# Fourth chunk of the input projection by seven half-sized products, with the first unit's exponentials, two weight sums and two tiles' taps moved behind it

## The reference

```python
h = rmsnorm(x, attn_norm_w)
proj = jnp.einsum('btd,de->bte', h, w_in)                 # 1024 -> 6400 columns
xin, bg, cg, q, k, v, g_conv, g_attn = jnp.split(proj, ...)
conv_out, conv_state = causal_short_conv(cg * xin, conv_prefix, conv_w)   # 3 taps in time
y_conv = bg * conv_out
q, k = rmsnorm(q, q_norm_w), rmsnorm(k, k_norm_w)
y_attn = window_attention(q, k, v, rel_bias, sinks)       # 16 heads, 2 of keys, window 128
merged = sigmoid(g_conv) * y_conv + sigmoid(g_attn) * y_attn
x = x + merged @ w_out
x = x + moe_ffn(rmsnorm(x, ffn_norm_w))                   # top 4 of 32 experts
```

## Time and profile before

| | |
|---|---|
| time of three runs | 1147.71, 1148.14 (median), 1148.73 us |
| the profiled execution: its own time | 1147.19 us |
| its span, first to last instruction | 1145.4 us |
| TensorE busy in the span | 1097.6 us (96%) |
| VectorE busy in the span | 437.5 us (38%) |
| mean granted TensorE clock | 0.993 |
| transfers | 444.36 MB, mean 388 GB/s |

### The profile page before, as it was taken

How to read it: one execution, slowest core, us unless ns; L and a number is a source line. 1 busy time by engine, 2 the same in 40 slices (tenths; PEclk the granted TensorE clock), 3 DMA queues, 4 the chain that set the end, 5 groups by cost and what they waited for, 6 DMA issues and landing times.

```text
span 1145.4 us, 15065 instructions
## 1 busy us (share of the span) xinstructions
PE 1097.6 (96%) x6055; PEld 497.1 (43%) x6055; DVE 437.5 (38%) x858; ACT 188.0 (16%) x398; POOL 88.4 (8%) x161
## 2 busy tenths in 40 slices
PE   9999999999999999999898999999999999999997
PEld 6689898543333333333333333333333333333332
DVE  4577786753433223233223232323232323232322
ACT  2133341221321101010101010101010101010101
POOL 1785215000000000000000000000000000000000
PEclk9999999999999999999999999999999999999999
DMA  9947629999999999999999999999999999999997
GB/s 313 314 128 186 210 85 353 416 357 425 400 420 426 419 432 431 430 433 431 433 433 429 434 430 433 435 428 434 429 434 431 431 434 429 435 429 434 425 423 287
DMA packets 53206, 444.36 MB, mean 388 GB/s; under 512 B 13101, under 2 KB 19373, under 8 KB 35741
## 3 DMA queue, kind: packets, MB, share of 16 engines
q1 hardware_dynamic: 46712, 435.83, 91.7%
q0 software_dynamic: 5600, 7.32, 2.4%
q10 hardware_dynamic: 852, 0.64, 0.2%
HBM read 439.78 MB, written 2.37 MB: 386 GB/s over the span
## 4 chain that ended last, share of the span: by engine, by line
PE 62%; DMA 37%; DVE 0%; issue 0%; ACT 0%; ACTq 0%; SPq 0%; DVEq 0%
PE pA L2051 32%; PE pB L2051 21%; DMA ring<-in_w_up 21%; DMA ring<-in_w_down 10%; PE pM L2051 6%; DMA area<-in_w_up 5%; PE pM L2054 1%; PE pA L2054 1%; DMA x<-in_x_prompt 1%; ACT area L1269 0%; DVE x L1898 0%; SPq L800 0%; DVE conv_row L1812 0%; DVE area L1973 0%; DVE x L1978 0%
## 5 line engine op out<-in xcount | busy, mean ns | idle before, releaser
L2051 PE MATMUL pA<-ring,hn 128*64 128x512 f32 x1536 | 352.6, 602 | 23.0 <-DMA ring<-in_w_up 23.0
L2051 PEld LDWEIGHTS pA<-ring,hn 128*64 128x64 f32 x1536 | 105.3, 137 | 218.8 <-issue 185.5
L2051 PE MATMUL pB<-ring,area 128*64 128x512 f32 (+2 forms) x784 | 171.5, 591 | 6.6 <-DMA ring<-in_w_down 5.8
L2051 PE MATMUL pA<-area,hn 128*64 128x512 f32 x512 | 119.3, 610 | 10.4 <-DMA area<-in_w_up 10.4
L2051 PE MATMUL pB<-area,ring 128*128 128x132 f32 (+2 forms) x928 | 126.4, 327 | 0.0
L2051 PEld LDWEIGHTS pB<-area,ring 128*128 128x128 f32 (+1 forms) x928 | 106.7, 175 | 18.2 <-issue 2.3
L2051 PEld LDWEIGHTS pB<-ring,area 128*64 128x64 f32 (+2 forms) x784 | 58.5, 136 | 101.2 <-issue 87.8
L1898 DVE TENSOR_TENSOR x<-pM,x 128x512 f32<-128x512 f32 x60 | 40.1, 691 | 147.7 <-PE pM L2051 147.7
L1257 ACT ACTIVATE area<-area 128x512 f32<-128x512 f32 x30 | 18.9, 631 | 385.2 <-DVE area L1881 385.2
L1812 DVE COPY conv_row<-pM 128x512 f32<-128x512 f32 x30 | 20.6, 686 | 146.0 <-PE pM L2051 146.0
L2051 PEld LDWEIGHTS pA<-area,hn 128*64 128x64 f32 x512 | 36.2, 139 | 74.5 <-issue 59.7
(11 more groups left out here) (348 smaller groups left out, 907.1 us busy)
## 6 DMA issues: line engine op xcount, KB each, us to landing
ring<-in_w_up SPq DMA_DIRECT2D x36, 4096.0 KB, 29.8
ring<-in_w_down SPq DMA_DIRECT2D x18, 4096.0 KB, 29.0
area<-in_w_up SPq DMA_DIRECT2D x12, 4096.0 KB, 30.2
ring<-in_w_up SPq DMA_DIRECT2D x16, 2048.0 KB, 13.4
area<-in_w_down SPq DMA_DIRECT2D x6, 4096.0 KB, 30.0
ring<-in_w_in SPq DMA_DIRECT2D x22, 1024.0 KB, 10.0
ring<-in_w_down SPq DMA_DIRECT2D x16, 1024.0 KB, 11.6
ring<-in_w_up SPq DMA_DIRECT2D x16, 1024.0 KB, 8.4
```

The lines of the kernel that those rows point to most:

```text
L2051: return pe.matmul(out, w, m, start=start, stop=stop, skip_group_check=True)
```

## The change

Chunk 4 (xin, first half) goes from four tiles to seven products. What goes with it:

```diff
-SEVEN = (3, 5, 6, 7, 9, 10, 11, 12)
-EARLY_SIDES = (3, 5)
+SEVEN = (3, 4, 5, 6, 7, 9, 10, 11, 12)
+EARLY_SIDES = (3, 4, 5)
...
-UNIT_STEPS = [(slot(3, 2), slot(3, 4), slot(3, 4), slot(3, 6), slot(3, 6), slot(5, 4), slot(5, 6)),
+UNIT_STEPS = [(slot(3, 2), slot(3, 4), slot(3, 4), slot(4, 0), slot(4, 2), slot(5, 4), slot(5, 6)),
...
-FIRST_TAP_STEPS = [15, 16, 17, 17, 30, 31, 32, 33]
-TAP_STEPS = [16, 17, slot(5, 0), slot(5, 0), 31, 32, 33, slot(9, 0)]
+FIRST_TAP_STEPS = [slot(4, 5), slot(4, 5), slot(4, 6), slot(4, 6), 30, 31, 32, 33]
+TAP_STEPS = [slot(4, 6), slot(4, 6), slot(5, 1), slot(5, 1), 31, 32, 33, slot(9, 0)]
...
-             5: (slot(3, 1), slot(3, 2), slot(3, 6), 14),
+             4: (slot(3, 1), slot(3, 2), slot(3, 4), slot(3, 6)),
+             5: (slot(4, 0), slot(4, 1), slot(4, 4), slot(5, 2)),
...
-    for n, what in ((15, "s_scores"), (16, "s_exp"), (17, "s_norm"), (slot(5, 3), "s_turn"), (slot(5, 5), "s_values")):
+    for n, what in ((slot(4, 2), "s_scores"), (slot(4, 4), "s_exp"), (slot(4, 6), "s_norm"), (slot(5, 3), "s_turn"), (slot(5, 5), "s_values")):
...
+                    if xin:
+                        out = quarter(cx[:, :, 2:], c, name)
+                        V.tensor_tensor(out, g, out, ALU.mult).then_inc(quarters_made, 1)
+                        dve.wait_ge(quarters_made, MADE_BEFORE[c] + ("c22", "c12", "c21").index(name) + 1)
```

More of the change, by code:

```diff
@@ L210, in plan @@
     after[2] += [("square", 0), ("qknorm", 0), ("bias_table", 0)]
-    for g, at in enumerate(((6, 7, 8, 9), (slot(3, 1), slot(3, 3), slot(3, 5), 14))):
+    for g, at in enumerate(((6, 7, 8, 9), (slot(3, 1), slot(3, 3), slot(3, 5), slot(4, 1)))):
         for n, what in enumerate((("q_sum", g), ("q_inverse", g), ("q_norm", (g, 0)), ("q_norm", (g, 1)))):
@@ L243, in plan @@
         after[SPLIT_STEPS[n]].append(("split", n))
+    assert not any(after[n] for n in range(len(TILES)) if TILES[n][1] in SEVEN)
     steps = [("anorm", 0), ("s_cols", 0)]
@@ L331, in counts @@
             for name in ("r1", "c11", "w", "c22", "c12", "c21"):
-                if name != "c11" or kind == "bg":
+                if name != "c11" or kind in ("bg", "xin"):
                     d += 1
@@ L347 @@
 counts()
+MADE_BEFORE = {4: 0, 8: 3 * (4 in SEVEN)}
 AFTER_XIN = [c for c in SEVEN if STEPS.index(("slot", (c, 0))) > STEPS.index(("sides", 4))]
@@ L600, in build @@
         tap_ready = sem("tap_ready")
+        quarters_made = sem("quarters_made")
         state_tapped = sem("state_tapped")
@@ L1110, in _ @@
                         act.wait_ge(kv_stored, 16 * 16)
-                    n = TILES.index(("xin", 4 if a < 4 else 8, a % 4, a))
-                    act.wait_ge(tile_free_dve, DVE_TILES[n] + 1)
+                    c = 4 if a < 4 else 8
+                    if c in SEVEN:
+                        act.wait_ge(quarters_made, MADE_BEFORE[c] + (2 if a % 4 < 2 else 3))
+                        act.wait_ge(tile_free_dve, DVE_READ[c, "c12"])
+                    else:
+                        act.wait_ge(tile_free_dve, DVE_TILES[TILES.index(("xin", c, a % 4, a))] + 1)
                     nc.scalar.activation(yc[:, a, 0:SEQ], cx[:, a, 0:SEQ], ACT.Copy,
@@ L1394, in place_of @@
                     return quarter(cx[:, :, 2:], c, name) if plain else g
+                xin = TILES[2 + 4 * (c - 1)][0] == "xin"
                 def times(name, g):
@@ L1399, in times @@
                     dve.wait_ge(tile_free_dve, DVE_READ[c, name])
-                    out = quarter(yc, c, name)
-                    link(V.tensor_tensor(out, g, out, ALU.mult))
+                    if xin:
+                        out = quarter(cx[:, :, 2:], c, name)
+                        V.tensor_tensor(out, g, out, ALU.mult).then_inc(quarters_made, 1)
+                        dve.wait_ge(quarters_made, MADE_BEFORE[c] + ("c22", "c12", "c21").index(name) + 1)
+                    else:
+                        out = quarter(yc, c, name)
+                        link(V.tensor_tensor(out, g, out, ALU.mult))
                 if s == 0:
@@ L1412, in seven @@
                         dve.wait_ge(sig_used, GATED[c - 1, "c21"])
+                    elif c - 1 in SEVEN:
+                        dve.wait_ge(tile_free_dve, DVE_READ[c - 1, "c21"])
                     read("r1", r1, t1, bank_y)
                 elif s == 2 and not (gated or plain):
-                    out = quarter(yc, c, "c11")
+                    if xin:
+                        dve.wait_ge(tile_free_act, ACT_DONE[c - 1, "c11"])
+                        dve.wait_ge(tile_free_dve, DVE_READ[c - 1, "c21"])
+                    out = quarter(cx[:, :, 2:] if xin else yc, c, "c11")
                     V.tensor_tensor(out, pairs_of(bank_x), out, ALU.mult).then_inc(tile_free_dve, 1)
```

## The result

| | before | changed |
|---|---|---|
| median of 21 runs | 1148.14 us | 1150.42 us (1148.27 to 1152.16) |
| ratio to before, 95% interval | | 1.0018 (1.0012 to 1.0024) |
| the profiled execution: time, span | 1147.19, 1145.4 us | 1149.08, 1147.3 us |

The change costs 2.1 us (0.0018 x 1148.14), between 1.4 and 2.8. The median of 1150.42 lies just inside the range (its upper end is 1150.5), well above the 1148.9 of the sum and above the 1149.8 at which the band of the likeliest case ended. The interval leaves out 1, so the loss is real; it is smaller than the 0.2% from which the prediction would have called it slower.

What follows compares the result with a forecast made beforehand. TensorE was taken as the bound around chunk 4. Saved 1.64, given back by VectorE 1.55, late moves 0.84: +0.75, so 1148.9 against the median of 1148.14; range 1147.0 to 1150.5.

Steps and rivals of the forecast that it cites:

- the likeliest case: Unit 0's moves land late and delay unit 1's bias step: 0 to +1.65, so 1148.1 to 1149.8; chance 0.42.
- three signs of being wrong: Load ahead of or behind the moves, product 6 starting before c22 is read, or r1 coming after 85.2.
- TensorE's saving: Chunk 4's products regrouped into longer runs: 14.64 falls to 13.00, 1.64 saved; bounds 1.84 and 1.04.
- VectorE eats it: Chunk 5: taps and a second sum delay c22, so product 6 begins at 95.31, leaving 0.09 of 1.64.
- Norm, scaling, issue: Unit 0's norm moves to 74.87, scaling follows 0.44 later, and the last of ten moves is issued at 83.24.
- The landing: Unit 0's last move, issued beside chunk 7's load, lands 5.2 later at 88.44, delaying the bias step from 87.60.
- The clock: In chunk 4's stretch TensorE's granted clock was 1.00, so it was taken to have nothing to give.
- Moves in time: Rival: VectorE eats the gain, unit 0's moves land by need; -0.1 to 0, 1148.1; chance 0.25.
- Gain through: Rival: chunk 5's product 6 isn't held by c22, so the 1.64 saving stays: 1146.5; chance 0.12.
- As late as SyncE's queue: Rival: unit 0's last move takes 7.1, landing at 90.34: +2.65, 1150.8; chance 0.10.
- VectorE's port holding up GpSimd's issues: Rival: a sum and two tiles' taps delay the last move's issue to 86.5: +4.0, 1152.2; chance 0.03.
- VectorE late in chunk 4: Rival: VectorE overruns its spare time in chunk 4, products and r1 about 1 late: 1149.0 to 1150; chance 0.08.

Runs made afterwards that it cites:

- load held: Against the changed kernel, chunk 7's load also waits until unit 0's ten moves have landed; ratio to the kernel before 1.0008, again 1.0013.
- norm back: Against the changed kernel, unit 0's norm put back ahead of the sample group's scores; ratio to the kernel before 1.0013.
- load later: Against the changed kernel, chunk 7's load issued 2 us later, behind product 0 of chunk 5; ratio to the kernel before 1.0026.
- norm back, taps later: Against the changed kernel, unit 0's norm ahead of the sample group's scores, taps of tiles 2 and 3 behind chunk 5's c22 and c12 reads; ratio to before 1.0020.
- TensorE kept at work: Against the changed kernel, TensorE repeats the sample group's four transpositions five times in all to fill its wait; median 1150.23 us, ratio to before 1.0027.

## Why the prediction held, and where it was short

None of the three signs of being wrong came: the load was issued among the moves (79.99), product 6 began at 97.70, behind the read of c22 that ended at 97.11, and r1 came at 84.87. The mechanism was right; that the time lay inside the range was partly luck, for the two sizes below put it 0.6 above the band of the case that was forecast, and 0.08 under the range's end.

- **TensorE's saving, 1.64.** Right: 1.63 at unit 1's scores, 1.63 at the end of the stretch once nothing eats it.
- **VectorE eats it.** Right in place and size: with the load held the bias step began at 87.34 (predicted 87.60, in an execution 0.29 early), and 0.10 to 0.15 was lost (without the drop of the clock) against a predicted gain of 0.09. The 7.71 from bias step to product 6 was 7.83. The wait of product 6 for c22 shows there (0.4); in the changed kernel product 6 didn't wait, because the slow products 4 and 5 ended later than VectorE.
- **Norm, scaling, issue.** Right: norm at 74.49 (74.87), scaling at 74.92, moves from 77.97 (78.05), the last at 83.19 (83.24). Exponentials no cause: they ended at 72.4.
- **The landing: the step that was mis-sized.** I took 5.2 as the middle between 4.4 and 6.1; it was 6.10, the row of the same block size. What I treated as a latency of each move hangs more on the load: issuing the last move 2 us earlier moved its landing by 0.3. The page "DMA: Bandwidth & Descriptors" of the Trainium skill (section "Queues, rings and completion order") has a rule that bears on this: a transfer's signal lands only after every earlier write of its DMA engine, in whatever queue. The traces neither confirm nor refute it: small transfers behind a load land late, as it would have them, but the load's own second half landed after 9.6, 9.6 and 9.3 in the three kernels (changed, norm back, load later), some 0.7 to 1.6 behind the last move, so the moves did not wait for all of the load.
- **The clock: a step that was missing.** "The clock has nothing to give" was read from a stretch without waits. It put nothing for what can follow a wait: 0.45 here, and 1.6 in one of four profiles with the load held.
- **The sum.** Predicted +0.75. The last move was issued 0.27 late once the earlier start of this execution is taken off, landed 0.90 later than taken, and the bias step followed 0.13 behind: +1.30; the longer way to product 6 +0.12; the clock +0.45. That makes 2.62 of the 2.75; 0.13 isn't assigned.
- **The rivals.** Moves in time: what the held kernel shows. Gain through: only when VectorE's work leaves chunk 5. As late as SyncE's queue (7.1): not reached, 6.10, but the clock brought the time near that case's 1150.8. VectorE's port holding up GpSimd's issues: no, ten issues in 5.80 beside the end of a sum and two tiles' taps, 5.77 before. VectorE late in chunk 4: no, it was idle for 1.03 ahead of r1.

## What to carry to other kernels

When an engine is sped up, what it releases moves too: a load that fell into an empty stretch now falls among small transfers whose landing somebody waits for, and here the load mostly set that landing, so either finish the small ones first or hold the load. A saving on the bound engine is only had if the work that pays for it goes where the helping engine is idle: here the same four taps cost the whole 1.64 in chunk 5 and nothing in chunk 6. A wait on TensorE can cost more than its length, for the clock may fall behind it, as it did here in some executions and not in others.

## What the runs showed that I had not expected

- TensorE idle for 2.4 us (changed kernel), and behind it some 3 us at a granted clock of 0.50; idle for 2.0 (norm back), and the same; idle for 1.6 (norm back, taps later) or for 0.9 behind steady work (TensorE kept at work), and the clock stayed at 1.00.
- The same three waits (0.3, 0.7, 0.4) with the clock at 1.00 in three profiles and at 0.52 to 0.63 behind them in a fourth, 1.6 us apart. Why one execution and not another stays open.
- A small transfer issued 1.1 us behind a 2 MB load (norm back, 81.14) took 7.84 to land, the one before it, 0.5 behind the load, 5.4; one issued 3.2 behind the load (changed kernel) took 6.10, those well ahead of it 1.8.
